# Block-local transposes on VectorE for the first five levels of a triangular inverse

## The reference, cut to what matters

```python
def step(state, inp):
    r_t, w_t, k_t, v_t, kk_t, a_t = inp
    sa = jnp.einsum('bhij,bhj->bhi', state, -kk_t)
    state = (state * w_t[:, :, None, :]
             + sa[..., :, None] * (kk_t * a_t)[:, :, None, :]
             + v_t[..., :, None] * k_t[:, :, None, :])
    y = jnp.einsum('bhij,bhj->bhi', state, r_t)
    return state, y
```

## Time and profile before

| | |
|---|---|
| median of 3 runs | 2096.63 us (2093.83 to 2096.66) |
| profiled run | 2091.61 us |
| its span | 2089.9 us |
| TensorE busy | 1863.5 us, 89% |
| VectorE busy | 718.6 us, 34% |
| ScalarE busy | 419.6 us, 20% |
| granted TensorE clock, mean | 0.942 of full speed |
| the stage of the eight units | from 261 to 640 us of the span |

### The profile page before, as it was taken

The page is one execution under the profiler, slowest core; times in us unless marked ns, Lnnn a source line. Parts: engine busy times, 40 slices in busy tenths (PEclk is TensorE's granted clock), DMA queues, the critical chain, the costliest instruction groups (busy, mean ns, idle before and its releaser), DMA issues.

```text
span 2089.9 us, 22236 instructions
## 1 busy us (share of the span) xinstructions
PE 1863.5 (89%) x8668; PEld 978.4 (47%) x8668; DVE 718.6 (34%) x1219; ACT 419.6 (20%) x857; POOL 67.3 (3%) x117
## 2 busy tenths in 40 slices
PE   6999089999998979999999985978889999999993
PEld 3443078888884443333333332467543333333331
DVE  2136976666663141111110104567223111111112
ACT  3015412222222111111111112234211111111110
POOL 3030000000000000000000001000000000000001
PEclk9999599999996989999999996998899999999997
DMA  9000000000002329999999988210025999999996
GB/s 276 0 0 0 0 1 1 0 0 0 0 1 89 154 105 418 429 429 428 428 429 428 429 332 306 96 41 1 1 81 207 428 429 428 429 429 427 429 429 259
DMA packets 68282, 459.72 MB, mean 220 GB/s; under 512 B 18749, under 2 KB 19911, under 8 KB 43655
## 3 DMA queue, kind: packets, MB, share of 16 engines
q1 hardware_dynamic: 55402, 433.77, 50.1%
q10 hardware_dynamic: 10524, 16.86, 2.2%
q0 software_dynamic: 2304, 8.39, 1.1%
HBM read 440.12 MB, written 18.87 MB: 220 GB/s over the span
## 4 chain that ended last, share of the span: by engine, by line
PE 77%; DVE 9%; DMA 7%; ACT 4%; issue 2%; ACTq 0%; POOL 0%; DVEq 0%; SPq 0%; POOLq 0%
PE bank L661 20%; PE bank L642 10%; PE bank L670 9%; PE bank L1711 7%; DMA ring<-in_moe_w_up_dram 5%; PE bank L1823 4%; PE bank L875 3%; PE bank L1831 3%; PE bank L1922 3%; PE bank L953 3%; PE bank L1839 1%; PE bank L1854 1%; PE bank L649 1%; DVE ring L1647 1%; PE bank L940 1%
## 5 line engine op out<-in xcount | busy, mean ns | idle before, releaser
L661 PE MATMUL bank<-ring,arena 128*64 128x512 f32 x2048 | 452.3, 594 | 10.8 <-DMA ring<-in_moe_w_up_dram 8.4
L582 DVE TENSOR_TENSOR arena<-arena,bank 64x512 f32<-64x512 f32 x64 | 67.0, 1046 | 700.7 <-ACT arena L452 700.7
L661 PEld LDWEIGHTS bank<-ring,arena 128*64 128x64 f32 x2048 | 148.0, 137 | 306.1 <-issue 303.6
L670 PE MATMUL bank<-ring,arena 128*64 128x512 f32 x1024 | 226.8, 595 | 1.4 <-ACT arena L462 1.4
L1711 PE MATMUL bank<-hT,ring 128*128 128x512 f32 x336 | 147.0, 600 | 1.3 <-issue 1.3
L670 PEld LDWEIGHTS bank<-ring,arena 128*64 128x64 f32 x1024 | 70.7, 137 | 134.8 <-issue 132.9
L452 ACT ACTIVATE arena<-bank 64x512 f32<-64x512 f32 x64 | 37.8, 591 | 419.9 <-PE bank L661 419.9
L642 PE MATMUL bank<-hT,arena 128*128 128x512 f32 x256 | 119.9, 612 | 1.5 <-DVE arena L522 1.5
L642 PE MATMUL bank<-xn,arena 128*128 128x512 f32 x256 | 119.7, 611 | 1.5 <-DVE arena L522 1.5
L1823 PE MATMUL bank<-ring 128*128 128x128 f32 x768 | 101.1, 284 | 5.4 <-DVE ring L1642 4.5
L1711 PEld LDWEIGHTS bank<-hT,ring 128*128 128x128 f32 x336 | 64.7, 193 | 83.1 <-issue 83.1
(11 more groups left out here) (323 smaller groups left out, 1963.5 us busy)
## 6 DMA issues: line engine op xcount, KB each, us to landing
ring<-in_moe_w_gate_dram SPq DMA_DIRECT2D x64, 2048.0 KB, 14.1
ring<-in_moe_w_up_dram SPq DMA_DIRECT2D x64, 2048.0 KB, 18.7
ring<-in_moe_w_down_dram SPq DMA_DIRECT2D x64, 2048.0 KB, 16.2
expert_rows<-arena ACTq DMA_DIRECT2D x128, 128.0 KB, 9.9
ring<-in_rec_w_in_dram SPq DMA_DIRECT2D x5, 2048.0 KB, 13.3
ring<-in_att_w_in_dram SPq DMA_DIRECT2D x3, 2048.0 KB, 11.9
ring<-in_rec_w_out_dram SPq DMA_DIRECT2D x2, 2048.0 KB, 10.3
ring<-in_att_w_out_dram SPq DMA_DIRECT2D x2, 2048.0 KB, 20.1
```

The lines of the kernel that those rows point to most:

```text
L582: nc.vector.tensor_tensor(by_chunk(hb[par * CAP:(par + 1) * CAP, :]), by_row(sg[0:CAP, par, :]), by_row(bank[par][CAP:2 * CAP, :]), ALU.mu ...
L661: mm = nc.tensor.matmul(bank[par][k * CAP:(k + 1) * CAP, :], xg[:, c, par * CAP:(par + 1) * CAP], W[k][:, c * FF:(c + 1) * FF], start=(c = ...
L670: mm = nc.tensor.matmul(bank[6 + par][h * CAP:(h + 1) * CAP, :], hT2[:, f, par * CAP:(par + 1) * CAP], W[:, f * D + h * 512:f * D + (h + 1 ...
```

## The change

At levels 0 to 4 the partial inverse has blocks of at most 32 rows. A VectorE `transpose` turns each 32x32 block in its place, so on such a matrix it gives the whole transpose. The change lets VectorE write `Tt[:, :, 0, :]` that way, one instruction for each half, behind a wait for the addition that wrote its source (`t_out`), and signals z(l+1) by a new semaphore `t_flip`. The transposes on TensorE and the copies on ScalarE stay for level 5 alone, where blocks have 64 rows. At level 0 the transpose of M goes, and with it the two masks and two additions that made the transposed form. ScalarE's copies for the previous unit and the exponentials for the next then stand together ahead of the two copies left. Counts in waits follow.

```diff
--- before.py
+++ after.py
@@ -187,7 +187,7 @@
             sem(n) for n in ("vcur_ready", "v_turned", "exp_ready", "prep_ready", "bk_turned", "bktok_ready"))
         m_done, m_out, z_done, z_out, t_done, t_out = (
             sem(n) for n in ("m_done", "m_out", "z_done", "z_out", "t_done", "t_out"))
-        t_turned, t_copied = sem("t_turned"), sem("t_copied")
+        t_turned, t_copied, t_flip = sem("t_turned"), sem("t_copied"), sem("t_flip")
         ident_ready, pool_filled, t_block, y_added = sem("ident_ready"), sem("pool_filled"), sem("t_block"), sem("y_added")
         rhs_done, rhs_out, u_done, u_out, ys_done, ys_out, loop_step = (
             sem(n) for n in ("rhs_done", "rhs_out", "u_done", "u_out", "ys_done", "ys_out", "loop_step"))
@@ -1226,7 +1226,7 @@
                 pool.wait_ge(v_turned, ft + 1)
                 copy_values(ft + 1)
                 add_outputs(ft)
-            pool.wait_ge(z_out, 2 * 8 * LEVELS)
+            pool.wait_ge(z_out, 2 * 8 * (LEVELS - 1))
             nc.gpsimd.memset(head_of, 0.0).then_inc(pool_filled, 1)
             nc.gpsimd.memset(head_sum, 0.0).then_inc(pool_filled, 1)
             pool.wait_ge(pool_filled, 3)
@@ -1395,18 +1395,16 @@
                     u_copy(*last, 0)
                     output_copies(*last, 0)
                     rhs_copy(*last, 1)
-                for l in range(1, LEVELS - 1):
-                    if last is not None and l == 2:
-                        output_copies(*last, 1)
-                    for q in range(2):
-                        act.wait_ge(t_turned, 10 * (2 * ft + d) + 2 * (l - 1) + q + 1)
-                        nc.scalar.activation(Tb[d][:, 4 * q:4 * q + 4, 0, :],
-                                             bank[4 + q][:, :].rearrange("p (k t) -> p k t", k=4),
-                                             ACT.Copy).then_inc(t_copied, 1)
-                    if last is not None and l == 1:
-                        u_copy(*last, 1)
-                    if nxt is not None and l == 2:
-                        exp_factors(*nxt)
+                if last is not None:
+                    u_copy(*last, 1)
+                    output_copies(*last, 1)
+                if nxt is not None:
+                    exp_factors(*nxt)
+                for q in range(2):
+                    act.wait_ge(t_turned, 2 * (2 * ft + d) + q + 1)
+                    nc.scalar.activation(Tb[d][:, 4 * q:4 * q + 4, 0, :],
+                                         bank[4 + q][:, :].rearrange("p (k t) -> p k t", k=4),
+                                         ACT.Copy).then_inc(t_copied, 1)
             act.wait_ge(sg_free, 8)
             exp_factors(0, 0)
             unit_copies(0, 0, None, (0, 1))
@@ -1625,7 +1623,9 @@
                                                 lvlmask[:, 1 - d, 0, :].unsqueeze(1).to_broadcast([P, 8, P]),
                                                 ALU.mult).then_inc(t_block, 1)
                     for q in range(2):
-                        dve.wait_ge(z_done, 14 * u + 2 * l + q + 1)
+                        if l == 0:
+                            break
+                        dve.wait_ge(z_done, 12 * u + 2 * (l - 1) + q + 1)
                         nc.vector.tensor_tensor(Zb[:, 4 * q:4 * q + 4, :], m4(bank[q][:, :]), four(lvlmask[:, d, l, :]),
                                                 ALU.mult).then_inc(z_out, 1)
                     if nxt is not None and l in (3, 4, 5):
@@ -1636,16 +1636,16 @@
                         k = 12 * u + 2 * (l - 1) + q + 1
                         if l == 0:
                             dve.wait_ge(t_block, u + 1)
-                            nc.vector.tensor_tensor(Tt[:, 4 * q:4 * q + 4, 1, :], Tt[:, 4 * q:4 * q + 4, 1, :],
-                                                    four(ident[:, :]), ALU.add)
-                            dve.wait_ge(z_out, 14 * u + q + 1)
-                            ins = nc.vector.tensor_tensor(Tt[:, 4 * q:4 * q + 4, 0, :], Zb[:, 4 * q:4 * q + 4, :],
+                            ins = nc.vector.tensor_tensor(Tt[:, 4 * q:4 * q + 4, 1, :], Tt[:, 4 * q:4 * q + 4, 1, :],
                                                           four(ident[:, :]), ALU.add)
                         else:
                             dve.wait_ge(t_done, k)
                             dst = Tt[:, 4 * q:4 * q + 4, 1, :]
                             ins = nc.vector.tensor_tensor(dst, m4(bank[2 + q][:, :]), dst, ALU.add)
                         ins.then_inc(t_out, 1)
+                        if l < LEVELS - 2:
+                            dve.wait_ge(t_out, 14 * u + 2 * l + q + 1)
+                            nc.vector.transpose(Tt[:, 4 * q:4 * q + 4, 0, :], Tt[:, 4 * q:4 * q + 4, 1, :]).then_inc(t_flip, 1)
                     if nxt is not None and l in (3, 4, 5):
                         prepare(2 * (l - 3) + 1, *nxt)
             for part in range(6):
@@ -1808,30 +1808,25 @@
 
                 def z(l):
                     for q in range(2):
-                        if l == 0:
-                            pe.wait_ge(m_out, 8 * u + 8)
-                        elif l == 1:
-                            pe.wait_ge(t_out, 14 * u + q + 1)
+                        if l < LEVELS - 1:
+                            pe.wait_ge(t_flip, 10 * u + 2 * (l - 1) + q + 1)
                         else:
-                            pe.wait_ge(t_copied, 10 * u + 2 * (l - 2) + q + 1)
+                            pe.wait_ge(t_copied, 2 * u + q + 1)
                         for i in range(4):
                             p = 4 * q + i
                             o = bank[q][:, i * P:(i + 1) * P]
-                            if l == 0:
-                                mm = nc.tensor.transpose(o, M[:, p, 0, :], ident[:, :])
-                            else:
-                                mm = nc.tensor.matmul(o, M[:, p, 0, :], Tt[:, p, 0, :], start=True, stop=True)
+                            mm = nc.tensor.matmul(o, M[:, p, 0, :], Tt[:, p, 0, :], start=True, stop=True)
                         mm.then_inc(z_done, 1)
 
                 def t(l):
                     for q in range(2):
-                        pe.wait_ge(z_out, 14 * u + 2 * l + q + 1)
+                        pe.wait_ge(z_out, 12 * u + 2 * (l - 1) + q + 1)
                         for i in range(4):
                             p = 4 * q + i
                             mm = nc.tensor.matmul(bank[2 + q][:, i * P:(i + 1) * P], Zb[:, p, :], Tt[:, p, 1, :],
                                                   start=True, stop=True)
                         mm.then_inc(t_done, 1)
-                    if l == LEVELS - 1:
+                    if l != LEVELS - 2:
                         return
                     for q in range(2):
                         pe.wait_ge(t_out, 14 * u + 2 * l + q + 1)
@@ -1856,7 +1851,6 @@
                     mm.then_inc(m_done, 1)
                 if last is not None:
                     solve(*last, 0)
-                z(0)
                 if last is not None:
                     outputs(*last, 0)
                 for l in range(1, LEVELS):
```

## The result

The changed kernel takes 2085.99 us against 2099.43 for the kernel before (medians of 13 runs each): the ratio is 0.9944, 95% interval 0.9931 to 0.9956, or 11.8 us less (9.2 to 14.5); the two medians themselves lie 13.4 apart. The profiled execution took 2084.23 us.

What follows compares the result with a forecast made beforehand. The path through each unit's TensorE and VectorE handovers was taken as the bound. Six middle units' 6.4, the last's 2.5 and the first's 0.4 sum to 9.3 us: profile 2082.3, median 2087.3, range 2075 to 2107.

Steps and rivals of the forecast that it cites:

- F: Duration of one VectorE flip of 128x512 elements, taken as 0.70 us, with ends at 0.427 and 1.226.
- Level 0: From the first mask of level 0 to t(1): 6.41 us against 7.17, a gain of 0.76.
- 1 to 2: From t(1) to t(2), other TensorE work covering the first flip: 6.85 us against 7.88, a gain of 1.03.
- 3 to 4: From t(3) to t(4), next unit's preparation in VectorE's order: mean 6.22 us against 5.45, a loss of 0.77.
- 4 to 5: From t(4) to t(5), masks no longer waiting for TensorE: 5.94 us against 5.59, a loss of 0.35.
- First unit: Unit without a previous unit's products and at a lower clock: gains and losses over its levels come to 0.4 us.
- All flips on the path: All ten flips of a unit delay it: gain 9.3 - 80 x (F - 0.70) us, gone at F = 0.82.
- One for one to the end: After the delta-rule stage everything hangs on its end: a microsecond gained or lost there is one at the end.
- the slow flip: Rival on VectorE between add and z: two passes, 1.226 us, give 2129.4; chance 0.13 above 0.87, 0.14 for 0.76 to 0.87.
- the cheap flip: Rival on VectorE: a single-source flip at 0.54 us gives 2074.5 us, at 0.427 gives 2065; chance 0.07.
- the transposes were free: Rival on TensorE: removing transposes gains nothing, level 3 and 4 losses stay, 8 us slower at most; 0.02 in each of two chances.
- The clock stayed at 1.00: Rival: TensorE's clock falls in levels 3 to 5; one fall a unit gives 2100.7 us, two 2114; chance 0.06.

Runs made afterwards that it cites:

- flip_twice: The changed kernel with every flip preceded by another of the same source into the mask buffer; stage 402.8 us against 354.2, ratio to the kernel before 1.0187.
- flip_merged: The changed kernel with one 1024-element flip for both halves instead of two of 512; stage 400.2 us against 354.2, ratio to the kernel before 1.0152.

## Why the prediction was right

It gave 9.3 us; the stage gave 10.6 and the runs 11.8 (9.2 to 14.5). The median of 2086.0 is 1.3 under the forecast of 2087.3, and that closeness is in part luck: the forecast was counted down from a median of 2096.6 of three runs, where thirteen gave 2099.4. Middle units are 44.68 and 45.39 us long, where 45.0 to 45.4 was said. Step by step, from the table:

- *F.* Taken as 0.70, measured 0.711, near the 0.72 that the Trainium skill ("VectorE: DVE Perf Modes", "The three transpose paths") led to. (The 0.272 us that the prediction has there for 128 elements should be 0.277, as 384 elements at 1.06 ns are 0.407; F becomes 0.72 either way.) By the formula this alone would have made the gain 8.4. The rows show one reason why it came out larger: the operation after a flip starts 0.63 to 0.64 later, where I had put 0.65, and the flip behind an addition that follows a flip starts 0.69 after it, not 0.72.
- *Level 0*: 0.81 for 0.76. *1 to 2*: 1.00 for 1.03. *2 to 3*: 0.22 for 0.24. *5 to 6*: 0.15 for 0.15.
- *3 to 4*: a loss of 0.73 for 0.77. *4 to 5*: 0.27 for 0.35, the largest error of a middle unit. Together 1.18 in a middle unit for 1.06.
- *First unit*: gaps shorter by 0.65 in all for 0.4. *Last unit*: 2.69 for 2.5.
- *All flips on the path*: 0.61 us for each added one (flip_twice), and 0.59 in the unit that grew from 44.68 to 50.62 us without a fall of the clock. All ten of a unit are on the path, as the formula has it. What a longer flip would cost was not measured; with the slope of 80 and 10.6 us at 0.711 the tie would stand at an estimated 0.84, not 0.82.
- *One for one to the end*: the start of the output projection moved from 677.38 to 662.69 us, 14.7, which is the 10.6 and the 4.1 of the clock behind it. After that the two profiles differ by what the last expert's clock and its queue do. The interval of the runs, 9.2 to 14.5, holds the stage's gain.

Of the rivals, the slow flip and the cheap flip fell with 0.711. That the transposes were free fell with level 1 to 2, where two flips took the place of transposes and copies, no VectorE work was taken away, and the gap is 1.00 us shorter. The clock stayed at 1.00 in the changed kernel's units after the first, as I had held likely, but the reason I gave (no new idle piece over 1.5 us) was luckier than it was good. The changed kernel idles in pieces of 0.5 to 1.0 us. flip_merged, with pieces of 2.06, did fall, but so did every second middle unit of flip_twice, whose longest piece is 1.36. The share of busy time of a whole unit doesn't separate them either: flip_twice kept 1.00 in units where TensorE is 79% busy, and flip_merged lost it in one with 82% (41.67 of 50.80).

Still open: why a given idle piece lowers the clock in one place and not in another. The unit at 362.65 has the same idle pieces of flip_merged as its neighbours and kept 1.00, half of flip_twice's middle units fell, and the last expert's 3.78 us wait lowered it in one profile and not in the other. I ran nothing that separates the causes.

## What to carry to other kernels

When work moves from a saturated engine to a half idle one, its worth is what it does to the order between one handover and the next, stage by stage; here the same edit gained 0.8 and 1.0 us at two levels and lost 0.7 and 0.3 at two others, and a sum over busy time could not have told. Look then at what else stands in the receiving engine's order: in the stage, moving the preparation out of the way was worth 2 us without the change and 10 with it, though the whole runs don't show that difference. And place the moved pieces where the engine waits for something anyway, with the first and last rounds of a loop looked at by themselves.

## What the runs showed of the hardware

- VectorE turns 128x512 float32 elements in 32x32 blocks in 0.711 us and 128x1024 in 1.245: 1.04 ns an element and 0.18 us once, against 1.06 and 0.14 for a two-operand operation. Four-byte data cost no second pass.
- Two VectorE operations in a row without a wait on each other start 0.60 us apart, with such a wait 0.72; behind a flip the next starts 0.63 later.
- TensorE's granted clock fell in units whose longest idle piece was 1.36 us (flip_twice, 0.97: t(4) took 3.33 us instead of 2.05) and 2.06 us (flip_merged, 0.90 and 0.93), and not in others with the same longest piece.
- TensorE can be made faster by useless work. In one profile of each kernel, 256 transposes in the idle pieces of flip_merged kept the clock at its upper level and took 18.3 us off the stage.
